# Second block, retention: outputs and state of one chunk in one slot with scores and keys of the next

## What is computed

```python
scores = jnp.einsum('bihd,bjhd->bhij', qc, kc) * inner_decay[None]
inner = jnp.einsum('bhij,bjhd->bihd', scores, vc)
cross = jnp.einsum('bihd,bhde->bihe', qc, state) * query_decay
new_state = state * chunk_decay + jnp.einsum('bjhd,bjhe->bhde', kc * key_decay, vc)
```

## Time and profile before

| what | value |
|---|---|
| median of 3 runs | 2513.19 us (2512.89 to 2514.77) |
| profiled execution, its own time | 2514.26 us |
| its span | 2512.9 us |
| PE busy | 2459.4 us, 98% |
| DVE, ACT, POOL busy | 67%, 46%, 58% |
| retentions 0 to 2 | about 1379 to 1549 us from the span's start |
| retention 3, with qa tiles | about 1552 to 1608 us |

### The profile page before, as it was taken

How to read it: one execution, slowest core, us unless ns; L and a number is a source line. 1 busy time by engine, 2 the same in 40 slices (tenths; PEclk the granted TensorE clock), 3 DMA queues, 4 the chain that set the end, 5 groups by cost and what they waited for, 6 DMA issues and landing times.

```text
span 2512.9 us, 35613 instructions
## 1 busy us (share of the span) xinstructions
PE 2459.4 (98%) x11970; PEld 2039.0 (81%) x11970; DVE 1691.4 (67%) x2889; ACT 1153.4 (46%) x2207; POOL 1469.0 (58%) x1157
## 2 busy tenths in 40 slices
PE   8999999999999999999999999889999999999999
PEld 6888888887888888887877887679888888888887
DVE  5337776188988879997267888767238445445988
ACT  6336663253333335445256666586234333333442
POOL 2133324456777769997426555374346666667986
PEclk9999999999999999999999999999999999999999
DMA  4254323213322246332223122220321222227342
GB/s 160 76 182 129 114 77 130 105 59 118 114 100 101 106 168 222 118 95 88 91 74 91 61 70 80 89 85 22 151 76 63 107 108 101 101 97 267 118 159 97
DMA packets 125045, 274.67 MB, mean 109 GB/s; under 512 B 11809, under 2 KB 33601, under 8 KB 124609
## 3 DMA queue, kind: packets, MB, share of 16 engines
q1 hardware_dynamic: 124864, 272.40, 31.7%
HBM read 198.42 MB, written 69.21 MB: 107 GB/s over the span
## 4 chain that ended last, share of the span: by engine, by line
PE 83%; DVE 5%; POOL 5%; issue 4%; ACT 2%; DMA 1%; SPq 0%; DVEq 0%; ACTq 0%; POOLq 0%
PE PS L794 9%; PE PS L1056 9%; PE PS L1058 9%; PE PS L1057 9%; PE PS L796 9%; PE PS L795 9%; PE PS L1092 4%; PE PS L1093 4%; PE PS L1094 4%; PE PS L1347 2%; PE PS L928 1%; PE PS L899 1%; PE PS L1327 1%; POOL Wl L3564 1%; POOL RG L3670 1%
## 5 line engine op out<-in xcount | busy, mean ns | idle before, releaser
L794 PE MATMUL PS<-Hh,Wl 128*128 128x512 f32 x1072 | 433.8, 405 | 13.6 <-DVE Hl L1489 9.4
L796 PE MATMUL PS<-Hh,Wh 128*128 128x512 f32 x1072 | 420.5, 392 | 0.0
L795 PE MATMUL PS<-Hl,Wh 128*128 128x512 f32 x1072 | 419.9, 392 | 0.0
L3564 POOL TENSOR_TENSOR Wl<-Wr,Wh 128x512 fp32r<-128x512 f32 (+1 forms) x158 | 210.1, 1351 | 331.7 <-ACT Wh L2600 331.5
L3670 POOL TENSOR_TENSOR RG<-SW,RG 128x512 fp32r<-128x512 f32 x120 | 184.1, 1534 | 212.2 <-ACT RG L2928 199.3
L3670 POOL TENSOR_TENSOR RG<-RW,RG 128x512 fp32r<-128x512 f32 x176 | 258.2, 1477 | 64.7 <-ACT RG L2928 63.5
L1058 PE MATMUL PS<-Hh,RG 128*128 128x512 f32 x640 | 249.0, 389 | 0.0
L1056 PE MATMUL PS<-Hh,RG 128*128 128x512 f32 x640 | 249.0, 389 | 0.0
L1057 PE MATMUL PS<-Hl,RG 128*128 128x512 f32 x640 | 249.0, 389 | 0.0
L794 PEld LDWEIGHTS PS<-Hh,Wl 128*128 128x128 f32 x1072 | 204.4, 191 | 52.9 <-POOL Wl L3564 11.2
L796 PEld LDWEIGHTS PS<-Hh,Wh 128*128 128x128 f32 x1072 | 202.2, 189 | 44.6
(11 more groups left out here) (449 smaller groups left out, 6064.4 us busy)
## 6 DMA issues: line engine op xcount, KB each, us to landing
hgscr<-GB SPq DMA_DIRECT2D x98, 256.0 KB, 2.0
RW<-in_wg SPq DMA_DIRECT2D x44, 512.0 KB, 3.7
RW<-in_wu SPq DMA_DIRECT2D x44, 512.0 KB, 4.6
R<-in_wd SPq DMA_DIRECT2D x40, 512.0 KB, 3.8
Wr<-in_wi SPq DMA_DIRECT2D x27, 512.0 KB, 3.5
Hl<-hgscr SPq DMA_DIRECT2D x16, 768.0 KB, 7.1
hgscr<-acc SPq DMA_DIRECT2D x36, 256.0 KB, 2.0
HC<-hgscr SPq DMA_DIRECT2D x12, 768.0 KB, 6.2
```

The costliest lines, as they stand in the source:

```text
L794: pe.matmul(ps(b), k.Wl[:, s, wc], xh[:, kx, sl], start=kk == 0, stop=False)
L795: pe.matmul(ps(b), k.Wh[:, s, wc], xl[:, kx, sl], start=False, stop=False)
L796: i = pe.matmul(ps(b), k.Wh[:, s, wc], xh[:, kx, sl], start=False, stop=kk == nk - 1)
L3564: i = pool.tensor_tensor(k.Wl[:, s, c], k.Wr[:, s, c], k.Wh[:, s, c].bitcast(F32), ALU.subtract)
```

## The change

- PE and DVE and ACT: chunk c's outputs and state move from slot 2c+2 to slot 2c+3, where the scores and turned keys of chunk c+1 follow them; the even slots are empty on PE. Outputs of chunk 7 are in slot 17. The turned outputs stay in slot 23 (21).
- The turned keys go to bank 6, the state's product keeps bank 7. Chunk 7's keys are no longer turned nor scaled (they were used for nothing).
- DVE: the state of chunk c-1 and `SD` of chunk c in slot 2c+1, the moments of chunk c-1 in slot 2c+2; moments of chunk 7, variance and the first two normalised chunks in slot 18 (17 in the last retention), the other six in the three slots behind.
- ACT: outputs of c-1 and then the keys of c in slot 2c+1.
- `least` and `other` of the bit search move from PSUM bank 6 to SBUF.

```diff
--- before.py
+++ after.py
@@ -495,6 +495,7 @@
     k.sx2, at = put("sx2", [128, 64], at)
     k.rx2, at = put("rx2", [128, 64], at)
     k.one, _ = put("one", [128, 1], late + 64 * T + 384)
+    k.rt_keys = k.PS[:, 512 * 6:512 * 6 + 128]
     k.rt_both = k.PS[:, 512 * 5:512 * 5 + 384].rearrange("p (h n) -> p h n", h=2)[:, :, 0:64]
     k.gq1, k.gq2 = k.sml[:, 100:101], k.sml[:, 101:102]
 
@@ -1219,9 +1220,9 @@
 
     def retention(j):
         y = j % 2
-        for c in range(8):
-            n = 8 * j + c
-            z, sl = c % 2, slice(128 * c, 128 * c + 128)
+
+        def scores(c):
+            n, sl = 8 * j + c, slice(128 * c, 128 * c + 128)
             take(3)
             if c == 0:
                 pe.wait_ge(*at("k_rot", j, 1))
@@ -1231,9 +1232,13 @@
                 r = slice(64 * h, 64 * h + 64)
                 m = pe.matmul(ps(3 + h, 128), k.KR[r, y, sl], k.QR[r, y, sl], start=True, stop=True)
             m.then_inc(*up(("full", 3), "rt_s", n))
-            take(7)
-            pe.transpose(ps(7, 128), k.KR[:, y, sl], ident).then_inc(*up(("full", 7), "rt_k", n))
-            yield
+            if c < 7:
+                if c:
+                    pe.wait_ge(*at("rt_kd", n - 1))
+                pe.transpose(k.rt_keys, k.KR[:, y, sl], ident).then_inc(*up("snap", "rt_k", n))
+
+        def outputs(c):
+            n, z, sl = 8 * j + c, c % 2, slice(128 * c, 128 * c + 128)
             take(5)
             if c:
                 pe.wait_ge(*at("rt_st", n - 1))
@@ -1248,8 +1253,16 @@
                 pe.wait_ge(*at("rt_kd", n))
                 pe.matmul(ps(7, 128), k.KD[:, z, :], k.VB[:, y, c, :], start=True,
                           stop=True).then_inc(*up(("full", 7), "rt_u", n))
+
+        for c in range(8):
+            if c:
+                outputs(c - 1)
+            scores(c)
             yield
-        for _ in range(6 if j < 3 else 4):
+            yield
+        outputs(7)
+        yield
+        for _ in range(5 if j < 3 else 3):
             yield
         take(3)
         pe.wait_ge(*at("rt_normed", j))
@@ -2266,7 +2279,8 @@
     kb = k.sml[:, 56:62].bitcast(I32)
     cand, cnt, thr, over = (k.sml[:, a:a + 6] for a in (44, 50, 64, 256))
 
-    under, least, other = k.sml[:, 264:270].bitcast(I32), ps(6)[:, 0:6], ps(6)[:, 16:22].bitcast(I32)
+    under, least, other = (k.sml[:, a:a + 6] for a in (264, 352, 360))
+    under, other = under.bitcast(I32), other.bitcast(I32)
     fix = k.sml[:, 280:288]
 
     def topk():
@@ -2354,13 +2368,43 @@
     def retention(j):
         y = j % 2
         gcol = k.cols[:, COL["g128"] + j:COL["g128"] + j + 1]
+
+        def state(c):
+            n, z = 8 * j + c, c % 2
+            dve.wait_ge(*at("rt_u", n))
+            if c:
+                dve.wait_ge(*at("rt_st", n - 1))
+            elif j == 0:
+                dve.wait_ge(*at("st_zero"))
+            for h in range(2):
+                r = slice(64 * h, 64 * h + 64)
+                sc = slice(64 * h, 64 * h + 64)
+                o = slice(512 * 7 + 64 * h, 512 * 7 + 64 * h + 64)
+                if c == 0:
+                    i = dve.tensor_copy(k.ST[r, 1 - z, sc], k.PS[r, o])
+                else:
+                    i = dve.scalar_tensor_tensor(out=k.ST[r, 1 - z, sc], in0=k.ST[r, z, sc], scalar=gcol[r, :],
+                                                 in1=k.PS[r, o], op0=ALU.mult, op1=ALU.add)
+                i.then_inc(*up(("free", 7) if h else "ret_v", "rt_st" if h else "rt_st0", n))
+
+        def moments(c):
+            n = 8 * j + c
+            for h in range(2):
+                if h == 0:
+                    dve.wait_ge(*at("rt_out", n))
+                dve.bn_stats(k.bst[:, 2 * c + h, :], k.YT[:, c, 64 * h:64 * h + 64]).then_inc(*up("ret_v", "rt_bn", n, h))
+                dve.wait_ge(*at("rt_bn", n, h))
+                dve.bn_aggr(k.bag[:, 2 * c + h, :], k.bst[:, 2 * c + h, :]).then_inc(*up("ret_v", "rt_bag", n, h))
+
         for c in range(8):
             n, z = 8 * j + c, c % 2
             sd = k.SD[:, z, :].rearrange("p (h n) -> p h n", h=2)
-            dve.wait_ge(*at("rt_s", n))
             if n == 0:
                 dve.memset(k.ST[:, :, :], 0.0).then_inc(*up("ret_v", "st_zero"))
                 dve.wait_ge(*at("dq"))
+            if c:
+                state(c - 1)
+            dve.wait_ge(*at("rt_s", n))
             if n >= 2:
                 dve.wait_ge(*at("rt_sd", n - 2))
                 dve.wait_ge(*at("rt_y", n - 2))
@@ -2368,29 +2412,12 @@
                               k.DQ[:, 256 * j:256 * j + 256].rearrange("p (h n) -> p h n", h=2), ALU.mult).then_inc(
                 *up(("free", 3), "rt_sd", n))
             yield
-            if c < 7:
-                dve.wait_ge(*at("rt_u", n))
-                if c:
-                    dve.wait_ge(*at("rt_st", n - 1))
-                elif j == 0:
-                    dve.wait_ge(*at("st_zero"))
-                for h in range(2):
-                    r = slice(64 * h, 64 * h + 64)
-                    sc = slice(64 * h, 64 * h + 64)
-                    o = slice(512 * 7 + 64 * h, 512 * 7 + 64 * h + 64)
-                    if c == 0:
-                        i = dve.tensor_copy(k.ST[r, 1 - z, sc], k.PS[r, o])
-                    else:
-                        i = dve.scalar_tensor_tensor(out=k.ST[r, 1 - z, sc], in0=k.ST[r, z, sc], scalar=gcol[r, :],
-                                                     in1=k.PS[r, o], op0=ALU.mult, op1=ALU.add)
-                    i.then_inc(*up(("free", 7) if h else "ret_v", "rt_st" if h else "rt_st0", n))
-            for h in range(2):
-                if h == 0:
-                    dve.wait_ge(*at("rt_out", n))
-                dve.bn_stats(k.bst[:, 2 * c + h, :], k.YT[:, c, 64 * h:64 * h + 64]).then_inc(*up("ret_v", "rt_bn", n, h))
-                dve.wait_ge(*at("rt_bn", n, h))
-                dve.bn_aggr(k.bag[:, 2 * c + h, :], k.bst[:, 2 * c + h, :]).then_inc(*up("ret_v", "rt_bag", n, h))
+            if c:
+                moments(c - 1)
             yield
+        if j < 3:
+            yield
+        moments(7)
         dve.wait_ge(*at("rt_bag", 8 * j + 7, 1))
         e = k.sml[:, 200:208].rearrange("p (c h) -> p c h", h=1).to_broadcast([128, 8, 2])
         dve.scalar_tensor_tensor(out=k.rsd[:, :].rearrange("p (c h) -> p c h", h=2), in0=e, scalar=10.0,
@@ -2407,7 +2434,7 @@
                 i = dve.tensor_scalar(k.YT[:, c, 64 * h:64 * h + 64], k.YT[:, c, 64 * h:64 * h + 64], k.bag[:, e, 0:1],
                                       k.rsd[:, e:e + 1], ALU.subtract, ALU.mult)
         i.then_inc(*up("ret_v", "rt_normed", j))
-        for _ in range(4 if j < 3 else 2):
+        for _ in range(3 if j < 3 else 2):
             yield
         for half in range(2) if j == 3 else ():
             sl = half_of(half)
@@ -3331,26 +3358,38 @@
 
     def retention(j):
         y = j % 2
-        for c in range(8):
-            n, z = 8 * j + c, c % 2
-            act.wait_ge(*at("rt_k", n))
-            if n >= 2:
-                act.wait_ge(*at("rt_kd", n - 2))
-                act.wait_ge(*at("rt_u", n - 2 if c != 1 or j == 0 else n - 3))
-            for h in range(2):
-                i = act.activation(k.KD[:, z, 64 * h:64 * h + 64], ps(7, 128)[:, 64 * h:64 * h + 64], ACT.Copy,
-                                   scale=col("kdec", 2 * j + h))
-            i.then_inc(*up(("free", 7), "rt_kd", n))
-            yield
+
+        def output(c):
+            n = 8 * j + c
             act.wait_ge(*at("rt_y", n))
             if c == 0 and j:
                 act.wait_ge(*at("rt_turn", j - 1))
             act.activation(k.YT[:, c, :].rearrange("p (h n) -> p h n", h=2), k.rt_both, ACT.Copy).then_inc(
                 *up(("free", 5), "rt_out", n))
+
+        for c in range(8):
+            n, z = 8 * j + c, c % 2
+            if c:
+                output(c - 1)
+            if c < 7:
+                act.wait_ge(*at("rt_k", n))
+                if c >= 2:
+                    act.wait_ge(*at("rt_kd", n - 2))
+                    act.wait_ge(*at("rt_u", n - 2))
+                elif j:
+                    act.wait_ge(*at("rt_u", n - 2 - 2 * c))
+                for h in range(2):
+                    i = act.activation(k.KD[:, z, 64 * h:64 * h + 64], k.rt_keys[:, 64 * h:64 * h + 64], ACT.Copy,
+                                       scale=col("kdec", 2 * j + h))
+                i.then_inc(*up("ret_a", "rt_kd", n))
+            yield
+            yield
+        output(7)
+        if j < 3:
             yield
         act.wait_ge(*at("rt_var", j))
         act.activation(k.rsd[:, :], k.rsd[:, :], ACT.Sqrt).then_inc(*up("ret_a", "rt_std", j))
-        for _ in range(6 if j < 3 else 4):
+        for _ in range(5 if j < 3 else 4):
             yield
         act.wait_ge(*at("rt_turn", j))
         for half in range(2):
```

## The result

| what | before | after |
|---|---|---|
| median of 16 runs each, on one chip | 2514.48 us (2512.01 to 2516.86) | 2519.14 us (2515.43 to 2522.36) |
| profiled execution, its own time | 2514.26 | 2518.58 |
| its span | 2512.9 | 2517.3 |
| PE busy | 2459.4, 98% | 2458.0, 98% |
| DVE, ACT, POOL busy | 67%, 46%, 58% | 68%, 46%, 58% |

The ratio is 1.0020 (95%: 1.0014 to 1.0027): 4.7 us slower, where I had forecast 3.0 slower. The lines of the code have moved: L1249 is now L1254, L1243 is L1248, L1257 is L1270, L830 and L840 are L831 and L841, L1459 is L1472; on DVE L2314, L2316 and L2321 are L2328, L2330 and L2335, `SD` is written at L2411, the root is L2423, L3391 and L2427, and the normalising groups are L2434.

A forecast was written before the change was run, and what follows sets the result against it. PE's own instructions bound retentions 0 to 2, with waits added in the last. Terms -0.3 + 4.2 - 0.9 - 1.3 + 1.3 = +3.0 us, from the median 2513.2 to 2516.2 us, 0.12% slower; range 2508 to 2522.

The forecast's parts named there:

- The first and third rival: First: DVE keeps ahead, 2507.7 us, chance 0.12. Third: nothing reaches PE, SD waits move to L1459, 2512.4 us, chance 0.06.
- The second: Rival: shared port holds DVE, L2321 waits too, both bits ahead of the turned outputs meet POOL; 2521.7 us, chance 0.27.
- PE's own instructions: On PE, the merged slot saves 0.00 us a chunk and four dropped key transposes save 0.08 each: -0.3 us.
- `SD` no longer waits: PE's L1243 loses its waits for SD: worth 0 in retentions 0 to 2; 2.1 us of waits go in retention 3.
- Retentions 0 to 2: PE waits at L1257's turned outputs for the late normalised group, 1.4 us three times: +4.2 us, bounds 0 and 7.5.
- I take 1.4 left: DVE time lost to POOL on the shared SBUF port ahead of the turned outputs: 1.4 us a retention, between 0 and 2.5.
- 0.84: DVE's queue before the last normalised group: search slot +1.25, chunk 6's moments +0.69, ACT-output wait gone -1.10; 0.84 us later.
- margin of 0.87: Before the change, last normalised group ends at 1547.74 and PE turns it at 1548.61: 0.87 us of room.
- -0.9: Retention 3, PE's first wait for L1459 (ends 1580.89): DVE idle 1.6 us goes, 0.7 given back for POOL; between -2.1 and +1.
- -1.3: Retention 3, L840 at 1591.14: its 1.29 us wait for L1459 goes, -1.3 us, at worst 0.
- +1.3: Retention 3, L840 at 1601.85: chunk 7's outputs come one slot later, so L1459 is later; +1.3 us, between 0 and +2.5.
- The clock: Retention 3, PE's clock loss of 1.8 us from the long wait at 1580.89 on stays: 0, between -1.8 and +1.8.

The follow-up runs named there:

- fourth kernel: Changed kernel with least and other back in PSUM and chunk 7's moments, root and normalising groups of retentions 0 to 2 one slot earlier; 2510.26 us, ratio 0.9981.
- first run: Kernel before the change, with only least and other of the bit search moved from PSUM to SBUF; 2521.42 us, ratio 1.0029.
- second kernel: Changed kernel with least and other back in PSUM bank 6 and the turned keys in bank 5 instead; 2515.60 us, ratio 1.0006.
- sixth kernel: As the second kernel, with chunk 7's moments and the root in slot 17 but the normalising groups kept in slots 18 to 21; 2515.10 us, ratio 1.0004.
- seventh: As the second kernel, with the normalising in three slots (18 to 20), in groups of 3, 3 and 2 chunks; 2522.36 us, ratio 1.0028.
- tenth: As the second kernel, with the outputs of chunk 7 alone back in slot 16; 2514.78 us, ratio 1.0001.

## Why the prediction was right in sign and place, and where it failed

- **Result.** Slower by 4.7 us against a forecast of 3.0, inside the range, and nearer the upper end. The first and third rival did not happen. The second has half of its condition (L2335 does wait, and all three operations can be blocked in one bit) but not its price: the blocks are not what PE waits for at L1270.
- **PE's own instructions,** -0.3. Without the wait and the stalls a retention is about 0.2 us shorter: the fourth kernel, which has neither, takes 53.32, 57.70 and 57.70 us in the first three rows of the table, before 53.52, 57.91 and 57.90. Three times that is -0.6, twice what I took.
- **`SD` no longer waits.** Right, and the first run shows its worth in the other direction: with the words in SBUF and the old order PE waits for it three times some 2 us.
- **Retentions 0 to 2,** +4.2, and no other gain or loss named. Measured, with the steps to the turned outputs from start to start: 1.72 + 1.71 + 1.74 + 0.55 + 0.56 - 0.6 = +5.7 (the table: 5.72). The waits stand where I put them. Their size was forecast at 1.4 and is 1.6 to 1.7; the stalls of 0.5 at the queries by the state in retentions 1 and 2 I had not forecast, and the second run shows them to be the port's.
- **The step that failed** is the reason given for 1.4 a retention: "I take 1.4 left" for the shared port ahead of the turned outputs, with "the wait for ACT's outputs ahead of chunk 7's moments goes: -1.10". By these terms 0.84 against a margin of 0.87 would leave no wait without the port; with the port taken out the wait stays (1.54). That wait for ACT did go, but a longer one for the root took its place, 1.32 instead of 0.36 in the change and 1.66 in the second kernel, since ACT's table load and square root, moved by a slot, stand behind its values and its copy. I had looked at DVE's queue and not at ACT's. From the root's end to PE's slot for the turn there were 1548.61 - 1537.88 = 10.73 us before and 1552.17 - 1544.87 = 7.30 after; the groups took 9.86 and 8.89 of them (1537.88 to 1547.74, 1544.87 to 1553.76). So 3.43 us of room were lost and 0.97 came back in the groups: 2.46, which is the margin of 0.87 and the 1.59 that DVE is late. The prediction's 0.84 + 1.4 = 2.24 comes near that sum by a wrong split, and the nearness is luck. The root's wait is not the whole of it either: in the sixth kernel it is back at 0.55 and PE waits 1.49.
- **The hand-over.** I counted the whole 0.87 us as margin; PE starts 0.15 after the last group ends, which makes the wait that much longer.
- **Retention 3,** -0.9, -1.3 and +1.3. The first was -1.98 (32.28 to 30.30), at the edge of its bounds, and it would be larger with the words in PSUM (another 1.5 in the second kernel). The other two came as forecast and cancel: L840/L841, 10.25 us behind the first wait before, is 8.86 behind it after (-1.39), and the late one 12.03 behind that instead of 10.71 (+1.32); in all 20.96 to 20.89. The gain at the first place stems from DVE's waits of the earlier trace rows, of which those at 1568.09 and 1574.23 are gone; I gave 0.7 back for the port there, and the L831 wait of 3.58 against 2.47 shows that it took 1.1.
- **The clock,** 0. Right: 0.91 in the same window in both.

What is settled: the turned outputs wait because of the slot in which the tail stands (moments of chunk 7, root and groups one slot later, against a turn in the same slot), and the words' cost is real, separate and about 3 us. Neither the root alone (sixth), nor fewer slots for the groups (seventh), nor the outputs alone (tenth) clears the wait; the whole tail a slot earlier does, with the words in either place. What stays open is POOL's share in it. The same four instructions of a group took 0.97 to 3.00 us, the long ones beside POOL's operations, and in the sixth and seventh kernel the groups took 1.20 and 1.83 us more in all, half and more than all of what the edit had won. That was seen, not tested; no run keeps the groups clear of POOL. The 1.1 us in the untouched part is unexplained as well.

## What to carry to other kernels

When work moves by a slot in programs that run in lock-step, follow the last stage's whole chain over every engine, with what each of them has queued ahead of it in the new slot: here a table load behind ACT's copies held DVE for 1.32 us, which no sum of DVE's own durations shows. Keep words of a few bytes where the operations on them don't wait for POOL: the 92 small operations of the search took DVE 30 us more as soon as their operands and results all lay in SBUF. And before a combined change is thrown away, run its parts as a square: here the stagger was worth 3.8 us, and the move of the words and the slot of the tail hid it.

## What the runs showed of the hardware

- A small operation of DVE can be blocked for nearly the whole of a long operation of POOL: in the kernel after, 2240 ns for L2335 beside POOL's L3903 (128x1024, from 1398.74 to 1401.13 us), where others of the same form take 172. The prediction had counted with 1.28 us for an operation of POOL. Three can be blocked in a row, each by another operation of POOL (1518.63 to 1523.13 us). L2335 has one input and one output in SBUF; with its output in PSUM the same instruction took at most 170 ns (second kernel). I had taken this one as optional. By the Trainium skill (page "SBUF — State Buffer", section "Who interferes with whom") tensor_scalar can enter a two-port mode and then contends as well, while an instruction with at most one SBUF input outside such a mode does not; the trace agrees with the first, since L2335 and the groups of L2434 (0.97 or 2.05 us for the same four instructions) are both of this kind.
- With one input in PSUM, none of the 31 runs of the first small operation and none of the 30 of the second was longer than 164 ns in the second kernel, beside the same work of POOL.
- Waits of PE of 1.5 to 1.6 us at the turned outputs were followed by the full clock (2.4 GHz) each time; those of 2.24 and 2.25 us in the seventh kernel by 3.4 us at 1.2 GHz, three of three. At L831 a wait of 2.47 or 2.48 was followed by such a stretch in the second, sixth and seventh kernel (0.91 over the 20 us from 1580 on) and not in the fourth or the tenth (1.00). In the kernel of the first experiment the wait of 2.15 us was, and in the kernel before one of 1.56 us at L830. So the length of the last wait alone does not tell, and a comparison of two traces has to look at the clock: such a stretch cost 1.5 us in the second kernel and 1.7 in the seventh.
- The table load for the square root took 1.28 us, every time (three in each trace; the root of retention 3 had none). The Trainium skill (page "ScalarE activation tables: per-element evaluation and per-set limits", section "What a function is on this engine") gives 1283 ns for it, and the trace agrees.
